# A decoder trunk with a mixture of experts: one ring of eight weight buffers, and the last norm read from PSUM

## The chip, the core and the metric

The kernel runs on one core of a Trainium2 chip. The metric is the device time of one execution in microseconds (us). The program has two layers, one after the other; all inputs and weights lie in HBM as float32, 509 MB are read in one execution.

## The reference, cut to what matters

Each layer has three sub-layers: a token mixer (short convolution beside latent attention), a cross-attention into 256 memory tokens, and a mixture of experts. After each of them the input is added and the sum is normalised. The change touches the third:

```python
D_MODEL, SEQ, DEPTH = 1024, 256, 2
N_EXPERTS, TOP_K, EXPERT_DIM = 64, 8, 256
DEEPNORM_ALPHA = (2 * DEPTH) ** 0.25

def layer_norm(x, g, b):
    mu = jnp.mean(x, axis=-1, keepdims=True)
    var = jnp.mean(jnp.square(x - mu), axis=-1, keepdims=True)
    return (x - mu) * lax.rsqrt(var + LN_EPS) * g + b

def experts(xt, gt):                     # gt: 8 of 64 gates per token are not zero
    hid = jax.nn.silu(jnp.einsum('btd,edf->btef', xt, w_gate)) * jnp.einsum('btd,edf->btef', xt, w_up)
    return jnp.einsum('btef,efd->btd', hid * gt[..., None], w_down)

def reference(x, mem, ...):
    for l in range(DEPTH):
        x = layer_norm(DEEPNORM_ALPHA * x + parallel_mixer(x, ...), ln1_g[l], ln1_b[l])
        x = layer_norm(DEEPNORM_ALPHA * x + memory_cross_attention(x, mem, ...), ln2_g[l], ln2_b[l])
        shared = (jax.nn.silu(x @ ws_gate[l]) * (x @ ws_up[l])) @ ws_down[l]
        x = layer_norm(DEEPNORM_ALPHA * x + experts(x, gates) + shared, ln3_g[l], ln3_b[l])
    return x
```

Every expert has a gate and an up matrix of 1024x256 and a down matrix of 256x1024, 1 MB each. All of them are read in each layer: 201 MB.

## The kernel before, in words

The order of the work is written out by hand, one instruction stream per engine, with semaphores between them. SP (SyncE) issues the weight loads, PE (TensorE) multiplies, ACT and DVE (VectorE) empty PSUM and do the norms, POOL (GpSimd) does small pieces of the norms.

**Dense stages.** The weights of the mixer, the cross-attention and the shared expert go through `ring`, six slots of 2 MB, in the order of `LOADS`; SP refills a slot when PE has filled the last bank that used it (`wait_read`). The 256 tokens are two blocks of 128 (`TT`), the 1024 channels eight chunks of 128 (`KC`).

**Expert stage.** The router puts the tokens of an expert into 32 slots per block. PE gathers a batch of four pairs of experts: one-hot matmuls of `x_hi` and `x_lo` (the input split into two parts) with `sel` give `xg`, L878. Then it goes pair by pair (`expert_body`, eight pairs in a body, four bodies): gate and up matmuls of both experts over eight chunks into `work[0]` (L952, 32 records a pair, 7.09 us); silu on ACT (L1169); times up and gate on DVE (L1568); two transposes (L969); down matmuls (L982); the result as `out_hi` and `out_lo` (L1173, L1579), and from these the scatter matmuls into `moe_sum`, four PSUM banks that hold the sum of the stage (L912). Gathers for the next batch and the scatter of the pair before stand between.

**Weights of the expert stage.** A pair needs three slots of 2 MB: gate and up of expert one, gate and up of expert two, down of both. In the ring these are slots 0, 1, 2 and 3, 4, 5 by turns. SP refills a gate and up slot when `gate_up_done` of the pair has come, and a down slot after `down_filled` (L474 and L480 are their issues). Each slot takes two DMAs of 1 MB: gate and up of one expert with one row of 8 KB per partition, down with two rows of 4 KB per partition. The first pair's gate and up weights lie in `ahead`, two more pieces of 2 MB in the arena, which are loaded while the dense stages end and are not used again in the layer.

**Around it.** `arena` is SBUF that stages share by views: `xg`, `ahead`, `hid` and, at its head, `gb`, the gain and bias rows of the norm. `X`, the input of the stage, has its own 8 KB per partition. After the last scatter `add_and_normalize` does, on DVE, four times `alpha * X + moe_sum` (L1239) and its statistics (L1246), then the aggregate (L1249); POOL makes the root and the shift (L578 to L594); ACT and DVE write the normalised halves `XN` (L1043, L1263), which PE transposes for the next layer (L688); DVE centres and scales (L1252) and writes the new X (L1273), which is the output after the last layer. In the loop head of the next layer ACT and DVE copy the transposed XN to `XT` (L1033, L1283). The causal mask of the attention is built on POOL once, at the start (L546, L561), and read at L1379.

## Time and profile before

| | us |
|---|---|
| three runs: median, lowest, highest | 1768.1, 1767.76, 1768.31 |
| the profiled execution | 1768.32 |
| its span, first to last instruction | 1766.5 |
| PE, PE weight loads, DVE, ACT, POOL busy | 1622.6, 909.8, 428.9, 279.9, 83.9 |
| mean granted TensorE clock | 0.984 |

The span is cut in 40 slices of 44.2 us. A digit of 9 for DMA says that the sixteen DMA engines were busy 90% of the slice or more; GB/s is what they moved. The two runs of slices near 417 GB/s are the expert stages of the two layers, 403 to 874 and 1277 to 1747 us. In the rows of a timeline the first number is the start, the second the length, in us from the span's start; in square brackets stands the idle time before and what ended it. In the chain of waits the first two numbers are the same, for merged pieces.

### The profile page before, as it was taken

The page shows a single profiled execution, that of the slowest core. Times are in us where ns is not written, and L with a number is a line of the kernel's source. Part 1 is how long each engine was busy: PE and PEld are TensorE (multiplying, and loading weights), DVE is VectorE, ACT ScalarE, POOL GpSimd, SP SyncE. Part 2 cuts the span into 40 slices and gives each one's busy share as a digit, 9 for nine tenths or more (in the row PEclk, how much of TensorE's full clock was granted, in tenths as well). Part 3 has the DMA queues.
Part 4 walks back from the last instruction along what each step waited for, and adds up shares of the span by engine and source line. Part 5 has one row for each costly group of instructions (what it writes and reads, how often), then busy time and mean ns, then how long its engine had stood idle before and what let it go on. Part 6 is the DMA issues. An engine that isn't in the chain of part 4 may idle for free.

```text
span 1766.5 us, 20370 instructions
## 1 busy us (share of the span) xinstructions
PE 1622.6 (92%) x7892; PEld 909.8 (52%) x7893; DVE 428.9 (24%) x865; ACT 279.9 (16%) x546; POOL 83.9 (5%) x121
## 2 busy tenths in 40 slices
PE   6999999989999999989789999999899999999985
PEld 4878677564333333333367885865633333333332
DVE  2141211152222222222322312011522222222224
ACT  1041011021111111111111310110211111111111
POOL 2000011040000000000010000200300000000001
PEclk8999999999999999999989999999999999999998
DMA  9174442446999999999940734333479999999994
GB/s 300 54 266 163 143 166 103 157 176 248 417 417 417 417 418 418 418 418 418 403 151 1 294 134 167 143 149 143 191 291 418 417 416 417 417 418 417 417 418 183
DMA packets 124811, 509.59 MB, mean 288 GB/s; under 512 B 12768, under 2 KB 16960, under 8 KB 91472
## 3 DMA queue, kind: packets, MB, share of 16 engines
q1 hardware_dynamic: 119808, 508.59, 72.3%
q10 hardware_dynamic: 4720, 0.02, 0.3%
q8 instruction: 46, 0.75, 0.2%
q0 software_dynamic: 224, 0.12, 0.1%
q14 instruction: 13, 0.11, 0.0%
HBM read 507.64 MB, written 1.05 MB: 288 GB/s over the span
## 4 chain that ended last, share of the span: by engine, by line
PE 65%; DMA 27%; DVE 3%; issue 2%; SPq 2%; ACT 1%; POOL 0%; ACTq 0%; DVEq 0%; POOLq 0%
PE work L662 37%; DMA ring<-in_w_up 26%; PE work L952 17%; PE work L982 4%; SPq L474 2%; PE work L878 2%; PE moe_sum L912 1%; PE moe_sum L866 1%; PE work L688 1%; PE work L756 0%; DVE stats L1246 0%; DMA par_all<-in_w_conv 0%; DVE X L1239 0%; DMA ring<-in_w_in 0%; PE work L777 0%
## 5 line engine op out<-in xcount | busy, mean ns | idle before, releaser
L952 PE MATMUL work<-ring,arena 128*64 128x512 f32 x1984 | 443.7, 599 | 62.9 <-DMA ring<-in_w_up 52.9
L952 PEld LDWEIGHTS work<-ring,arena 128*64 128x64 f32 x1984 | 157.1, 138 | 307.2 <-issue 305.1
L662 PE MATMUL work<-XT,ring 128*128 128x256 f32 x1280 | 278.2, 379 | 1.1 <-DVE arena L1379 1.1
L662 PEld LDWEIGHTS work<-XT,ring 128*128 128x128 f32 x1280 | 242.7, 190 | 35.7 <-DVE arena L1379 1.9
L982 PE MATMUL work<-ring,arena 128*64 128x512 f32 x1024 | 233.9, 598 | 1.3 <-DVE arena L1572 1.3
L662 PE MATMUL work<-ring,arena 128*128 128x512 f32 (+1 forms) x336 | 140.6, 579 | 8.3 <-DVE arena L1422 3.4
L1579 DVE TENSOR_TENSOR out_lo<-work,out_hi 128x512 fp32r<-128x512 f32 x128 | 88.6, 692 | 231.5 <-ACT out_hi L1173 231.5
L1568 DVE SCALAR_TENSOR_TENSOR arena<-arena,slot_gate,work 128x256 f32<-128x256 f32 x64 | 30.7, 480 | 449.3 <-ACT arena L1169 449.3
L982 PEld LDWEIGHTS work<-ring,arena 128*64 128x64 f32 x1024 | 68.0, 136 | 134.0 <-issue 111.3
L1173 ACT CAST out_hi<-work 128x512 fp32r<-128x512 f32 x128 | 75.1, 587 | 213.0 <-PE work L982 213.0
L1169 ACT ACTIVATE arena<-work 128x256 f32<-128x256 f32 x64 | 24.7, 385 | 523.2 <-PE work L952 523.2
L662 PEld LDWEIGHTS work<-ring,arena 128*128 128x128 f32 x336 | 63.3, 190 | 82.7 <-issue 72.9
L878 PE MATMUL work<-sel,x_hi 128*128 128x256 f32 x288 | 90.1, 335 | 1.6 <-DVE arena L1544 1.4
L878 PEld LDWEIGHTS work<-sel,x_hi 128*128 128x128 f32 x288 | 54.0, 188 | 66.6 <-issue 63.7
L578 POOL TENSOR_SCALAR small<-small 128x1 f32<-128x1 f32 x20 | 6.8, 338 | 1602.7 <-DVE small L1249 1544.9
L878 PE MATMUL work<-sel,x_lo 128*128 128x256 f32 x288 | 75.6, 285 | 0.0
L912 PE MATMUL moe_sum<-out_hi,selT 32*128 32x512 f32 x512 | 64.6, 494 | 1.8 <-DVE out_lo L1579 1.6
L912 PEld LDWEIGHTS moe_sum<-out_hi,selT 32*128 32x128 f32 x512 | 24.5, 181 | 63.6 <-issue 62.6
L662 PE MATMUL work<-ring,XT 128*128 128x384 f32 (+2 forms) x192 | 49.6, 421 | 7.9 <-DMA ring<-in_w_in 5.3
L1150 ACT COPY arena<-work 128x512 f32<-128x512 f32 x72 | 42.3, 587 | 85.8 <-PE work L878 85.8
L662 PE MATMUL work<-arena,ring 128*128 128x256 f32 x256 | 55.8, 380 | 0.0
L662 PE MATMUL work<-memT,ring 128*128 128x256 f32 x256 | 55.6, 379 | 0.0
(204 smaller groups left out, 1168.9 us busy)
## 6 DMA issues: line engine op xcount, KB each, us to landing
ring<-in_w_down SPq DMA_DIRECT2D x128, 1024.0 KB, 19.1
ring<-in_w_gate SPq DMA_DIRECT2D x124, 1024.0 KB, 15.2
ring<-in_w_up SPq DMA_DIRECT2D x124, 1024.0 KB, 17.4
ring<-in_w_in SPq DMA_DIRECT2D x28, 1024.0 KB, 12.4
ring<-in_w_mix_out SPq DMA_DIRECT2D x8, 1024.0 KB, 12.7
ring<-in_w_xk SPq DMA_DIRECT2D x8, 1024.0 KB, 6.2
ring<-in_w_xq SPq DMA_DIRECT2D x8, 1024.0 KB, 7.8
ring<-in_w_xv SPq DMA_DIRECT2D x8, 1024.0 KB, 6.2
```

The lines of the kernel that those rows point to most:

```text
L474: sp.dma_start(dst[:, h * SLOT // 2:(h + 1) * SLOT // 2].rearrange("p (k n) -> p k n", k=KC), w[at].rearrange("o p k f -> (o p) k f")).the ...
L662: mm = pe.matmul(dst, a, b, start=(k == 0), stop=(k == len(pairs) - 1))
L688: mm = pe.transpose(w[:, (c * TT + t) * P:(c * TT + t + 1) * P], XN[:, t, 2 * i + c::KC], ident[:, :])
L878: mm = pe.matmul(dst[:, :, t, :], part[:, t, c * P:(c + 1) * P], src, start=(part is x_hi), stop=(part is x_lo))
L912: mm = pe.matmul(moe_sum[2 * (q % TT) + half][:, :], selT[rows, b, k, :], part[rows, half * BANK:(half + 1) * BANK], start=False, stop=Fal ...
L952: mm = pe.matmul(work[0][rows, :], xg[b][:, c, k * P + e * TT * SLOTS:k * P + (e + 1) * TT * SLOTS], wgu[:, :, c, :], start=(c == 0), stop ...
L982: mm = pe.matmul(w[rows, :], hidT[:, c, rows], wd[:, c, half * BANK:(half + 1) * BANK], start=(c == 0), stop=(c == 1))
L1150: act.copy(xg[b][:, c, :], work[bank][:, :]).then_inc(gather_ready[0], 1)
L1169: act.activation(act_gate, work[0][:, 0:EXPERT_DIM], ACT.Silu).then_inc(silu_ready, 1)
L1173: act.copy(out_hi[:, half * BANK:(half + 1) * BANK], work[1 + half][:, :]).then_inc(hi_ready[half], 1)
L1568: dve.scalar_tensor_tensor(out=hid, in0=act_gate, scalar=slot_gate[:, b, k:k + 1], in1=work[0][:, EXPERT_DIM:2 * EXPERT_DIM], op0=ALU.mult ...
L1579: dve.tensor_tensor(out_lo[:, cols], work[1 + half][:, :], out_hi[:, cols].bitcast(F32), ALU.subtract).then_inc(lo_ready[half], 1)
```

## The change

The eight buffers (six of `ring`, two of `ahead`) form one ring of `UNITS`. A pair of experts takes three units in turn: gate and up weights of both experts for contraction chunks 0 to 3, the same for chunks 4 to 7, down of both. SP refills a unit when its reader is through, and `gate_up_done` counts halves of a pair. To have `ahead` free of other use for the whole stage, `xg`'s second buffer goes to the head of the arena (where `gb` lies, so ln3's rows are loaded after the last gate and up matmul) and a buffer `xg_more`; `hid`, `hidT` and `gated` share `hidden`, silu writes `hid` in place, and ACT waits for two DVE reads of `gated` before the fourth silu of a batch; `X` lies where `out_hi` and `out_lo` are; the mask lies in the arena and POOL builds it in each layer after the `rankT` transposes. Gates and shared hidden values are divided by alpha, so `moe_sum` holds the sum over alpha: PE adds `x_hi` and `x_lo` by identity matmuls (`add_input`, behind pairs 4 to 7 of the first body), the statistics are read from PSUM with the epsilon divided by alpha squared, ACT writes all halves of XN from PSUM, and DVE centres from PSUM, block 1 first.

The diff, cut; the hunk that moves the mask's memset and two selects into POOL's layer loop is among what is left out.

```diff
...
 RING = 6
+UNITS = 8
...
-RING_USES = BODY_PAIRS // 2
+RING_USES = 3 * BODY_PAIRS // UNITS
...
-        xg = [view(2 * K + b * 4 * K, KC, BATCH * P) for b in range(2)]
-        ahead = view(6 * K, 2, SLOT)
...
+        xg_first, xg_second = view(2 * K, KC, BATCH * P), view(0, KC // 2, BATCH * P)
+        xg = [[xg_first[:, c, :] for c in range(KC)],
+              [(xg_second if c < KC // 2 else xg_more)[:, c % (KC // 2), :] for c in range(KC)]]
+        ahead = view(6 * K, UNITS - RING, SLOT)
+        unit = [ring[:, u, :] if u < RING else ahead[:, u - RING, :] for u in range(UNITS)]
+        hid = hidden[:, 0:EXPERT_DIM]
+        hidT = hidden[:, EXPERT_DIM:].rearrange("p (c s) -> p c s", c=2)
+        gated = hidden[:, :].rearrange("p (k t) -> p k t", k=BATCH)
+        mask = view(0, 3 * P)
...
+            def wait_unit_read(m, pairs, halves):
+                q, part = divmod(m - UNITS, 3)
+                if part == 2:
+                    alone(sp, down_filled[1], pairs + (q + 1))
+                else:
+                    alone(sp, gate_up_done, halves + (2 * q + part + 1))
...
+                def load_unit(m, pair_first):
+                    u, part = m % UNITS, m % 3
+                    for i in range(2):
+                        if part == 2:
+                            dst = unit[u][:, i * SLOT // 2:(i + 1) * SLOT // 2].rearrange("p (k n) -> p k n", k=2)
+                            src = e_down[bass.ds(pair_first + i, 1)].rearrange("o p k d -> (o p) k d")
+                        else:
+                            dst = unit[u].rearrange("p (w e k n) -> p w e k n", w=2, e=2, k=KC // 2)[:, i]
+                            src = (e_gate, e_up)[i][bass.ds(pair_first, 2), :, part * (KC // 2):(part + 1) * (KC // 2), :
+                                                    ].rearrange("e p k f -> p e (k f)")
+                            dst = dst.rearrange("p e k n -> p e (k n)")
+                        sp.dma_start(dst, src).then_inc(slot_loaded[u], 16)
+                first = [sp.snap(l * EXPERTS + 2 * q) for q in range(BODY_PAIRS)]
+                for m in (0, 1):
+                    wait_read(l, len(LOADS) - RING + m)
+                    load_unit(m, first[0])
                 b, n = job("xpT", JOBS["xpT"] - 1)
                 alone(sp, filled[b], l * BANK_USES[b] + n)
...
-                def load_pair(l, i, j, pairs, gate_up=True):
-                    pair_first = sp.snap(l * EXPERTS + i * 4 + 2 * j)
-                    for e in range(2):
-                        if gate_up:
-                            sp.wait_ge(gate_up_done, pairs + (j + 1))
-                            load_gate_up(ring[:, 3 * j + e, :], pair_first + e, slot_loaded[3 * j + e])
-                    sp.wait_ge(down_filled[1], pairs + (j + 1))
-                    load_down(3 * j + 2, pair_first)
...
+                load_unit(6, first[2])
+                for m in (2, 3):
+                    wait_read(l, len(LOADS) - RING + m)
+                    load_unit(m, first[m // 3])
+                load_unit(7, first[2])
+                for m in (4, 5):
+                    wait_read(l, len(LOADS) - RING + m)
+                    load_unit(m, first[m // 3])
+                def load_body(body, pair_firsts, units):
+                    pairs, halves = sp.snap((body + 1) * BODY_PAIRS), sp.snap((body + 1) * (2 * BODY_PAIRS))
+                    for m in units:
+                        wait_unit_read(m, pairs, halves)
+                        load_unit(m, pair_firsts[m // 3])
+                load_body(base, first, range(UNITS, UNITS * RING_USES))
                 sp.reg_mov(more, 1)
-                sp.reg_mov(start, 2)
+                sp.reg_mov(start, 1)
...
                 with sp.Fori(0, more) as r:
+                    with sp.Fori(start, BODIES) as i:
+                        firsts = [sp.snap(l * EXPERTS + i * (2 * BODY_PAIRS) + 2 * q) for q in range(BODY_PAIRS)]
+                        load_body(sp.snap(base + r * BODIES + i), firsts, range(UNITS * RING_USES))
                     sp.reg_mov(start, 0)
                     alone(sp, routing_ready, l + 1)
                     sp.reg_load(more, rounds[0:1, bass.ds(l, 1)])
+                done = sp.value_load(bodies[0:1, bass.ds(l + 1, 1)], min_val=0, max_val=4 * BODIES * DEPTH)
+                alone(sp, gate_up_done, sp.snap((done + 1) * (2 * BODY_PAIRS)))
                 load_ln(l, ln3_g, ln3_b, 2)
...
+                def add_input(i):
+                    t, half = i // 2, i % 2
+                    for part in (x_hi, x_lo):
+                        rows = in_rows(part, t)[:, half * (BANK // KC):(half + 1) * (BANK // KC), :]
+                        pe.matmul(moe_sum[i][:, :].rearrange("p (q c) -> p q c", c=KC), ident_r[:, :], rows,
+                                  start=False, stop=False, skip_group_check=True)
...
+                    loaded = [pe.snap((body * RING_USES + (l + 1) * DENSE_USES) * 32), pe.snap(body * (RING_USES * 32))]
...
-                        b, k, slot = q // BATCH, q % BATCH, 3 * (q % 2)
-                        arrived = 32 * (q // 2 + 1)
-                        if first and q == 0:
-                            pe.wait_ge(ahead_loaded, l * 64 + 64)
-                        else:
-                            for e in range(2):
-                                pe.wait_ge(slot_loaded[slot + e], loaded + arrived)
+                        b, k = q // BATCH, q % BATCH
+                        def wait_unit(m):
+                            u = m % UNITS
+                            pe.wait_ge(slot_loaded[u], loaded[u // RING] + 32 * (m // UNITS + 1))
+                            return unit[u]
                         if k == 3:
                             pe.wait_ge(gated_ready, batch + (b + 2))
-                        for c in range(KC):
...
-                        mm.then_inc(gate_up_done, 1)
+                        for part in range(2):
+                            wgu = wait_unit(3 * q + part).rearrange("p (w e k n) -> p w e k n", w=2, e=2, k=KC // 2)
+                            for c in range(part * (KC // 2), (part + 1) * (KC // 2)):
+                                if k == 0:
+                                    pe.wait_ge(gather_ready[c % 2], (batch + b) * (KC // 2) + (c // 2 + 1))
+                                for e in range(2):
+                                    rows = slice(e * TT * SLOTS, (e + 1) * TT * SLOTS)
+                                    mm = pe.matmul(work[0][rows, :],
+                                                   xg[b][c][:, k * P + e * TT * SLOTS:k * P + (e + 1) * TT * SLOTS],
+                                                   wgu[:, :, e, c % (KC // 2), :], start=(c == 0), stop=(c == KC - 1))
+                            mm.then_inc(gate_up_done, 1)
...
+                        if first and q >= BODY_PAIRS - 4:
+                            add_input(q - (BODY_PAIRS - 4))
...
+                    if which == 2:
+                        if t == 1:
+                            act.wait_ge(centred_ready, l + 1)
+                        for half in range(2):
+                            act.activation(XN[:, t, half * BANK:(half + 1) * BANK], moe_sum[2 * t + half][:, :],
+                                           ACT.Identity, scale=ln_rstd[:, t:t + 1], bias=ln_shift[:, t:t + 1]
+                                           ).then_inc(norm_ready[half], 1)
+                        continue
...
+                            act.wait_ge(gate_up_done, halves + 2 * (BODY_PAIRS + q + 1))
+                            if k == 3:
+                                act.wait_ge(selT_ready, batch + (b + 2))
+                                act.wait_ge(slot_gate_ready, batch + (b + 2))
+                            act.activation(hid, work[0][:, 0:EXPERT_DIM], ACT.Silu).then_inc(silu_ready, 1)
...
-                    w = wait_filled(dve, l, stage, i) if stage else moe_sum[2 * t + half]
-                    ins = dve.scalar_tensor_tensor(out=X[:, t, cols], in0=X[:, t, cols], scalar=ALPHA, in1=w[:, :],
-                                                   op0=ALU.mult, op1=ALU.add)
                     if stage:
-                        take(ins, l, stage, i)
-                    else:
-                        step(ins)
-                    settle()
-                    step(dve.bn_stats(stats[:, t, 6 * half:6 * half + 6], X[:, t, cols]))
+                        w = wait_filled(dve, l, stage, i)
+                        take(dve.scalar_tensor_tensor(out=X[:, t, cols], in0=X[:, t, cols], scalar=ALPHA, in1=w[:, :],
+                                                      op0=ALU.mult, op1=ALU.add), l, stage, i)
+                        settle()
+                    step(dve.bn_stats(stats[:, t, 6 * half:6 * half + 6],
+                                      X[:, t, cols] if stage else moe_sum[2 * t + half][:, :]))
...
-                def centre(t):
-                    return dve.scalar_tensor_tensor(out=centred[:, t, :], in0=X[:, t, :],
-                                                    scalar=moments[:, 2 * t:2 * t + 1], in1=gb[:, 0, :],
-                                                    op0=ALU.subtract, op1=ALU.mult)
-                if which == 2:
-                    dve.wait_ge(ln_loaded, (l * 3 + 3) * 32)
-                    settle()
-                    step(centre(0))
...
+                dve.wait_ge(ln_loaded, (l * 3 + 3) * 32)
+                settle()
+                for t in (1, 0):
+                    if t == 0:
+                        for half in range(2):
+                            dve.wait_ge(norm_ready[half], l * 6 + 7)
+                    for half in range(2):
+                        cols = slice(half * BANK, (half + 1) * BANK)
+                        ins = dve.scalar_tensor_tensor(out=centred[:, t, cols], in0=moe_sum[2 * t + half][:, :],
+                                                       scalar=moments[:, 2 * t:2 * t + 1], in1=gb[:, 0, cols],
+                                                       op0=ALU.subtract, op1=ALU.mult)
+                        if t == 1 and half == 1:
+                            tell(ins, centred_ready, l + 1)
+                        else:
+                            step(ins)
+                settle()
                 for t in range(TT):
...
+                    dve.wait_ge(ln_rstd_ready, l * 6 + (5 + t))
+                    tell(dve.scalar_tensor_tensor(out=X[:, t, :], in0=centred[:, t, :], scalar=ln_rstd[:, t:t + 1],
+                                                  in1=gb[:, 1, :], op0=ALU.mult, op1=ALU.add),
+                         (layer_done if t == 0 else ln_applied), (l + 1 if t == 0 else l * 3 + 4))
...
```

## Rows read from the trace of the kernel before

**Rows 1.** The page, 40 slices: DMA busy tenths, GB/s

```profile
DMA  9174442446999999999940734333479999999994
GB/s 300 54 266 163 143 166 103 157 176 248 417 417 417 417 418 418 418 418 418 403 151 1 294 134 167 143 149 143 191 291 418 417 416 417 417 418 417 417 418 183
```

**Rows 2.** Waits, whole span: who waited for whom, us in total, times, longest

```profile
PE work L952 <- DMA ring<-in_w_up: 52.9, 39, 2.8
```

**Rows 3.** The chain of waits: pairs 0 and 4 of the first layer

```profile
403.24 7.04 PE work L952 x32
...
457.99 7.02 PE work L952 x32
```

**Rows 4.** Timeline, 398 to 436 us, PE: pairs 0 and 1

```profile
403.17 7.09 PE L952 MATMUL work<-arena 128*64 128x512 f32 x32
...
416.62 7.09 PE L952 MATMUL work<-ring,arena 128*64 128x512 f32 x32
```

**Rows 5.** Timeline of SP's queue, 340 to 520 and 830 to 856 us

```profile
397.37 19.57 SPq L480 DMA_DIRECT2D ring<-in_w_down  x4
423.89 0.34 SPq L474 DMA_DIRECT2D ring<-in_w_gate  x1
...
845.95 1.54 SPq L449 DMA_DIRECT2D arena<-in_ln_g  x1
```

**Rows 6.** DMA, 400 to 440 us, 40 slices of 1 us

```profile
GB/s 430 406 426 418 111 0 0 0 0 0 0 0 0 0 0 0 0 156 373 430 410 422 307 0 66 139 426 451 418 410 401 426 451 401 426 393 430 418 397 422
```

**Rows 7.** DMA of 527.5-530.9, 617.86-621.26, 517.6-525.8 and 884-892 us, in turn

```profile
DMA packets 359, 1.41 MB, mean 413 GB/s; under 512 B 20, under 2 KB 20, under 8 KB 355
...
DMA packets 356, 1.39 MB, mean 408 GB/s; under 512 B 19, under 2 KB 19, under 8 KB 354
...
DMA packets 469, 3.40 MB, mean 415 GB/s; under 512 B 52, under 2 KB 52, under 8 KB 57
...
DMA packets 1455, 3.11 MB, mean 388 GB/s; under 512 B 47, under 2 KB 47, under 8 KB 1454
```

**Rows 8.** Timeline, 860 to 900 us: the end of the first layer

```profile
860.70 7.09 PE L952 MATMUL work<-ring,arena 128*64 128x512 f32 x32 [1.04 <-DMA ring<-in_w_up]
...
869.95 3.65 PE L982 MATMUL work<-ring,arena 128*64 128x512 f32 x16
...
877.38 0.69 DVE L1239 SCALAR_TENSOR_TENSOR X<-X,moe_sum 128x512 f32<-128x512 f32 x1 [1.68 <-PE moe_sum L912]
...
880.14 0.21 DVE L1249 BATCH_NORM_AGGREGATE small<-stats 128x2 f32<-128x12 f32 x1
...
881.87 0.24 POOL L594 TENSOR_SCALAR small<-small 128x1 f32<-128x1 f32 x1
...
887.42 0.81 ACT L1043 ACTIVATE arena<-X,small 128x512 f32<-128x512 f32 x1 [4.47 <-POOL small L594]
...
888.60 1.28 DVE L1273 SCALAR_TENSOR_TENSOR X<-arena,small 128x1024 f32<-128x1024 f32 x1
```

**Rows 9.** Timeline of the second layer's stage: first, last gate/up, last norm

```profile
1276.78 7.09 PE L952 MATMUL work<-arena 128*64 128x512 f32 x32
...
1734.24 7.09 PE L952 MATMUL work<-ring,arena 128*64 128x512 f32 x32 [1.04 <-DMA ring<-in_w_up]
...
1762.15 1.28 DVE L1273 SCALAR_TENSOR_TENSOR X<-arena,small 128x1024 f32<-128x1024 f32 x1
```

**Rows 10.** Groups by line: busy us, mean ns | idle before, what ended it

```profile
L878 PE MATMUL work<-sel,x_hi 128*128 128x256 f32 x288 | 90.1, 335 | 1.6 <-DVE arena L1544 1.4
L1102 ACT ACTIVATE arena<-work 128x512 f32<-128x512 f32 x8 | 4.8, 598 | 50.5 <-PE work L662 50.5
```

**Rows 11.** The mask: its selects by line (POOL), its first reader in time

```profile
L561 POOL TENSOR_SCALAR_AFFINE_SELECT mask<-mask 128x128 f32<-128x128 f32 x2 | 0.5, 294 | 0.0
...
120.07 2.52 DVE L1379 TENSOR_TENSOR arena<-work,mask 128x384 f32<-128x384 f32 x4 [0.95 <-PE work L762]
```

163 lines of the change are left out of this document (63 added, 100 removed).

## The prediction

> **What bounds the kernel now.** I read the slices of the page first [rows 1]: in slices 10 to 18 and 30 to 38 the DMA digit is 9 and the rate lies at 416 to 418 GB/s; these are the two expert stages. In the dense stages the rate is 54 to 300 and PE carries the time. So an expert stage is a stream of weights, and the question is when the stream starts, how fast it runs, and what is left to do when it ends. The table of waits agrees: PE waits only 52.9 us in all for a weight load, in 39 short waits [rows 2], so PE lags the stream by little: four pairs of experts take PE 457.99 - 403.24 = 54.75 us when nothing is missing, 13.7 us each [rows 3], and the stream needs 6.29 MB / 417 GB/s = 15.1 us each. 32 pairs are 438 us of PE and 483 us of stream; the stage ends early enough only because eight 2 MB pieces are there at its start.
>
> The start is where the stream loses time. The last dense slot is refilled from 397.37 on, and the next issue that brings new weights in earnest is at 423.89, after the second pair's gate and up matmuls; between them one w_down piece goes out when the first pair's down matmuls end [rows 4, 5]. The DMA view of 400 to 440 us shows it: 0 GB/s from 405 to 417, one burst, another hole at 423 to 425, then full rate [rows 6]. The reason is in the code: the two pieces that hold the first pair's gate and up weights lie in the arena (`ahead`) and are never used again, so the ring works with six.
>
> **Part 1, the ring of eight.** The change keeps the two arena pieces in the ring and cuts a pair into three units of 2 MB: gate and up of both experts for contraction chunks 0 to 3, the same for 4 to 7, and down. SP can refill unit 0 when the first half of the first pair's matmuls is through: they start at 403.17 and take 7.09 us, so half is at 406.7, and SP issues 0.18 us after such an end (416.62 + 7.09 = 423.71 to 423.89) [rows 4, 5], at 406.9. The later units come free faster than the stream takes them (PE 13.7 us for three, stream 15.1 or more), so from there it need not pause. Before the last matmul half, 87 units have to land (8 of the 96 are there, the last down follows).
>
> How long is a unit? Gate and up now come as rows of 4 KB where they were 8 KB; down was and is 4 KB. The stream of before has both kinds by turns. Of seven stretches with 4 KB packets nearly alone the first ran at 413 GB/s and the last at 408, the others between; of the 8 KB stretches beside them the slowest ran at 415 [rows 7]. A stretch holds some packets of its neighbour, which pulls both kinds together, so I take 410 for 4 KB, below the middle: 2.097 MB / 410 = 5.115 us a unit, against 5.03 at the stream's 417. The ends are 415 (5.05 us, 5.4 us less a layer) and 408 (5.14 us, 2.2 us more). What stands around the stream I take from before: from the issue at 423.89 to the last gate and up landing at 860.70 [rows 5, 8] are 436.8 us with 86 pieces of 5.03 (432.6), so 4.2 us are first latency and last landing. After: 406.9 + 87 x 5.115 + 4.2 = 856.1. Then only half of the gate and up matmuls is left, 3.55 us: end at 859.65, against 860.70 + 7.09 = 867.8. That is 8.1 us earlier. The last down unit lands at 861.2; its matmuls came 2.16 us after the gate and up matmuls (867.79 to 869.95) [rows 8], now at 861.8, so it is just in time, by 0.6 us; what it is late beyond that, the end is late too.
>
> In the second layer the stage starts at 1276.78 and the last matmuls at 1734.24 [rows 9]: 1276.78 + 3.55 + 0.18 + 445.0 + 4.2 = 1729.7, end 1733.3, against 1741.3: 8.0 us.
>
> The Trainium skill (DMA: Bandwidth & Descriptors, Anatomy of one DMA) fits a transfer as 2.0 us plus bytes over 436 GB/s, with nothing for the size of the rows. By it the unit would not grow, and the sum would be that of rival B, 1729.6. The trace leans against it, by little.
>
> **Part 2, the input through PE.** Eight matmuls of 128x512 per layer with an identity are added behind pairs 4 to 7 (of 32). The nearest rows are the gathers, 335 ns for 256 columns [rows 10]: 8 x 2 x 0.335 = 5.4 us at most, 2 to 3 likely since such records overlap. All of it lies beside a stream that is already the slower side; by pair 4 PE leads by 4 x 1.4 = 5.6 us against the refill that the stream needs next. Cost 0; if that cover were gone, up to 5.4 us a layer. The strided moving operand has no row here; twice the price would still fit.
>
> **Part 3, the last norm.** Before: four times add (0.69) and statistics (0.69), then centre, scale, final; from the first add at 877.38 to the end of the last L1273 at 889.88 are 12.5 us [rows 8]; at the end of the kernel it is the same chain, ending at 1763.43 [rows 9]. After, on DVE: four statistics straight from PSUM 2.8, two aggregates 0.45, two halves of centring for block 1 from PSUM 1.35, the same for block 0 1.35, two L1273 2.55: 8.5 with the gaps. ACT must do block 0's XN before the second centring: its POOL chain ends 1.8 us after the aggregate (880.35 to 882.11) [rows 8], so at 880.8, and two halves from PSUM at 0.6 (as L1102) [rows 10] end at 882.0, the moment DVE wants them. So 3.9 us less. Bounds: 0 if PSUM reads or POOL hold it, 4.7 if ACT's XN, which ends at 888.23 now and at 883.5 then, were the gate; but it is DVE that, after its last L1273 [rows 8], must come round to the next layer and copy half of XT before PE can go on, so I take DVE's 3.9. At the end of the kernel the output DMA moves by the same.
>
> **Part 4, the small moves.** The ln3 rows are loaded only when the last gate and up matmul is done, 859.7, instead of from 845.95 on [rows 5]; two 0.5 MB loads behind the last down unit land near 867, and DVE wants them at 880.7 - 8.1 = 872.6: hidden by 5 us. The next layer's six dense loads stand behind them on SP, some 8 us later than now, six units of 5.4 us at the 388 GB/s of such rows [rows 7]: the first is there by 873. PE needs it after the transposes of XN, which follow ACT's at 888.23 [rows 8] less 12 us, so not before 876; and the dense stages draw less than the queue gives in every slice [rows 1]. Cost 0; the cover is 3 us, and if it failed, its lack would be the cost. The mask is made once per layer on POOL (two selects of 0.29 us and a memset) once rankT is transposed, before the q and k projections, and DVE reads it at 120.07 [rows 11]: hidden by PE work of tens of microseconds. ACT's two more waits before the fourth silu of a batch are for DVE work that precedes 7 us of PE matmuls: 0.
>
> **Sum.** 8.1 + 8.0 + 2 x 3.9 = 23.9 us off the profiled execution's 1768.3 (span 1766.5 and 1.8 around it; the median 1768.1 is the same number): 1744.
>
> **Rivals.**
> A, as worked out: 1744, its own range 1737 to 1752.
> B, rows of 4 KB cost nothing: unit 5.03, 87 x 0.085 = 7.4 us less a layer, 1744.4 - 14.8 = 1729.6. For it: the two kinds lie within 2% and their windows are blurred. PE does not stop it: 403.2 + 31 x 13.7 + 3 loop turns of 1.5 us reach the last pair by 832.
> C, the stream gains as in A but the new norm gives nothing, because ACT and DVE take turns at PSUM and each waits for the other: 1752.
> D, the other side. A gate or up load now takes every other 4 KB of a matrix, for two experts by turns; if HBM or the queue serves that worse, it hits 58 of the 87 units. Priced with the only slower rate in the trace, 388 GB/s for the 2 KB rows of w_in [rows 7]: 5.405 us, 58 x 0.29 = 16.8 us a layer more, 4.8 more than all gains: 1744 + 33.6 = 1778. It decides from 5.32 us a unit, 394 GB/s. Against it: down loads also read rows 0.5 MB apart by turns, and keep 408 or more [rows 7].
>
> **How the numbers follow.** A 0.57, B 0.13, C 0.15, D 0.10, and 0.05 for something between. About 0.2% (3.5 us) is what a measurement of this kernel can tell from no change. A, B and C are all far beyond it: faster 0.87; D slower 0.10; 0.03 between. The range runs from B's time to beyond C's, 1728 to 1757, and leaves out D.
>
> **What would show it.** In the trace after: no hole at 405 to 417 and none behind it; 409 to 411 GB/s through slices 10 to 18 (417 means B, under 395 D); PE waits of 1.5 us twice in a pair or less; the last gate and up matmul at 859 to 860; about 8.5 us from the end of the scatters to the last L1273 (12 means C). The prediction is wrong if a hole stays at the start of the stage, or if the stream's rate leaves 408 to 416.

## The result: 1.0% faster, three quarters of the forecast gain

| | median us (lowest to highest) | ratio to before, 95% interval |
|---|---|---|
| before, on the same chip | 1768.2 (1767.76 to 1769.27) | |
| changed | 1750.59 (1750.04 to 1752.47) | 0.990 (0.9887 to 0.9914) |
| forecast | 1744 | 0.986 |

The gain is 17.6 us where 23.9 were forecast; between the two profiled executions it is 18.2 us (spans 1766.5 and 1748.3).

The page of the changed kernel comes first: the span, two of the rows of slices, and the packets. It is to be laid beside [rows 1].

```profile
span 1748.3 us, 20830 instructions
...
DMA  9164343448999999999870734434599999999995
GB/s 298 60 258 175 125 164 127 145 164 337 409 409 409 409 409 409 410 410 410 333 282 1 293 140 168 145 128 166 192 359 409 409 409 409 410 410 409 409 410 232
DMA packets 157587, 509.65 MB, mean 292 GB/s; under 512 B 12768, under 2 KB 16960, under 8 KB 157008
```

Through both stages the rate is 409 to 410 where it was 416 to 418. The bytes are the same; now nearly every packet is under 8 KB. The tenth slice, in which the first stage begins, moved 337 GB/s for 248 before, because the stream starts earlier. The DMA view of 400 to 440 us, one number per us, answers to [rows 6]:

```profile
GB/s 426 422 426 352 8 0 0 70 127 430 414 410 426 414 430 328 315 369 328 332 356 410 434 406 418 414 422 410 406 414 401 406 401 422 410 406 397 426 410 406
```

The two holes of 12 and 2 us are gone; what is left is 404 to 409, until the first refill (issued at 406.79) arrives. New is a dip, 315 to 369 GB/s at 415 to 421. The next rows are the timeline of the first layer's stage: its start, its last gate and up half, its last down matmuls, and then the turn to the next layer; they answer to [rows 3, 8].

```profile
402.96 7.09 PE L976 MATMUL work<-ring,arena 128*64 128x512 f32 x32
...
859.25 3.65 PE L976 MATMUL work<-arena,xg_more 128*64 128x512 f32 x16 [0.97 <-DMA arena<-in_w_up]
...
863.15 0.35 SPq L459 DMA_DIRECT2D arena<-in_ln_g  x1
...
865.07 3.65 PE L1006 MATMUL work<-arena,hidden 128*64 128x512 f32 x16
...
872.48 1.29 DVE L1286 BATCH_NORM_STATS2 stats<-moe_sum 128x6 f32<-128x512 f32 x2 [1.66 <-PE moe_sum L937]
...
875.85 0.21 POOL L578 TENSOR_SCALAR small<-small 128x1 f32<-128x1 f32 x1
...
877.36 1.41 DVE L1309 SCALAR_TENSOR_TENSOR arena<-moe_sum,small,arena 128x512 f32<-128x512 f32 x2 [0.49 <-ACT arena L1074]
877.45 1.45 ACT L1074 ACTIVATE arena<-moe_sum,small 128x512 f32<-128x512 f32 x2 [0.19 <-POOL small L610]
878.89 2.48 DVE L1319 SCALAR_TENSOR_TENSOR X<-arena,small 128x1024 f32<-128x1024 f32 x2
...
885.67 0.18 DVE L1337 COPY par<-par_all 128x17 f32 x1 [4.30 <-issue]
886.00 1.90 DVE L1328 TENSOR_SCALAR XT<-work,par 128x256 f32<-128x256 f32 x4 [0.16 <-DVE par L1337]
...
887.05 8.43 PE L678 MATMUL work<-ring,XT 128*128 128x384 f32 x21 [2.76 <-DVE XT L1328]
```

The second layer, from timelines of its start and end, beside [rows 9]:

```profile
1266.55 5.80 PE L976 MATMUL work<-ring,arena 128*64 128x512 f32 x26
...
1722.97 3.65 PE L976 MATMUL work<-arena,xg_more 128*64 128x512 f32 x16 [0.97 <-DMA arena<-in_w_up]
...
1736.19 1.29 DVE L1286 BATCH_NORM_STATS2 stats<-moe_sum 128x6 f32<-128x512 f32 x2 [1.65 <-PE moe_sum L937]
...
1742.60 2.48 DVE L1319 SCALAR_TENSOR_TENSOR X<-arena,small 128x1024 f32<-128x1024 f32 x2
```

From these ends the gain adds up. In the kernel before, the next layer's L662 resumed at 896.74.

| stretch | before | after | gain | forecast |
|---|---|---|---|---|
| stage 1, first gate/up matmul to end of the last | 464.6 | 459.9 | 4.7 | 8.1 |
| its end to the next layer's matmuls | 28.95 | 24.15 | 4.8 | 3.9 |
| dense part of layer 2 | 380.0 | 379.5 | 0.5 | 0 |
| stage 2 | 464.6 | 460.1 | 4.5 | 8.0 |
| its end to the end of the span | 25.2 | 21.7 | 3.5 | 3.9 |
| start of stage 1 | 403.2 | 403.0 | 0.2 | 0 |
| sum | | | 18.2 | 23.9 |

So the norm gave what was forecast, and a little more; the stage gave only 4.7 of 8.1.

### The profile page after: what moved, and what is told of

The parts are those of the page before. It is cut to its first block, busy times and chain, and to the rows that moved or that the text cites. A ratio compares the mean times of both kernels' runs of the same rounds, so it can differ in the third digit from the quotient of the medians.

```text
span 1748.3 us, 20830 instructions
## 1 busy us (share of the span) xinstructions
PE 1631.3 (93%) x7908; PEld 888.5 (51%) x7909; DVE 420.4 (24%) x858; ACT 282.4 (16%) x550; POOL 80.1 (5%) x124
## 3 DMA queue, kind: packets, MB, share of 16 engines
HBM read 507.64 MB, written 1.05 MB: 291 GB/s over the span
## 4 chain that ended last, share of the span: by engine, by line
PE 59%; SPq 29%; DMA 5%; issue 3%; DVE 2%; ACT 1%; DVEq 0%; ACTq 0%; POOL 0%; POOLq 0%
PE work L678 38%; SPq L502 29%; PE work L976 9%; PE work L1006 5%; DMA arena<-in_w_up 4%; PE work L894 2%; PE moe_sum L937 2%; PE moe_sum L882 1%; PE work L704 1%; PE moe_sum L929 0%; PE work L772 0%; DMA par_all<-in_w_conv 0%; DMA ring<-in_w_in 0%; PE work L993 0%; PE work L793 0%
## 5 line engine op out<-in xcount | busy, mean ns | idle before, releaser
L976 PE MATMUL work<-ring,arena 128*64 128x512 f32 x1152 | 260.0, 597 | 16.2 <-DMA ring<-in_w_up 12.9
L1006 PE MATMUL work<-ring,hidden 128*64 128x512 f32 x768 | 175.4, 599 | 1.0 <-DVE hidden L1620 1.0
L976 PEld LDWEIGHTS work<-ring,arena 128*64 128x64 f32 x1152 | 77.7, 136 | 169.8 <-issue 139.9
L1616 DVE SCALAR_TENSOR_TENSOR hidden<-hidden,slot_gate,work 128x256 f32<-128x256 f32 x64 | 30.8, 481 | 440.9 <-ACT hidden L1210 440.9
L1210 ACT ACTIVATE hidden<-work 128x256 f32<-128x256 f32 x64 | 24.6, 385 | 514.7 <-PE work L976 514.7
L976 PE MATMUL work<-ring,xg_more 128*64 128x512 f32 x384 | 87.1, 595 | 17.6 <-DMA ring<-in_w_up 17.6
L1006 PEld LDWEIGHTS work<-ring,hidden 128*64 128x64 f32 x768 | 51.0, 136 | 100.5 <-issue 85.1
L976 PE MATMUL work<-arena 128*64 128x512 f32 x384 | 86.8, 597 | 6.6 <-DMA arena<-in_w_up 5.9
L578 POOL TENSOR_SCALAR small<-small 128x1 f32<-128x1 f32 x20 | 4.8, 238 | 1505.3 <-DVE small L1290 1446.8
L976 PEld LDWEIGHTS work<-ring,xg_more 128*64 128x64 f32 x384 | 26.5, 137 | 76.1 <-issue 48.0
L1006 PE MATMUL work<-arena,hidden 128*64 128x512 f32 x256 | 58.5, 599 | 0.0
## 6 DMA issues: line engine op xcount, KB each, us to landing
ring<-in_w_mix_out SPq DMA_DIRECT2D x8, 1024.0 KB, 12.5
```

The lines of the kernel that those rows point to most:

```text
L976: mm = pe.matmul(work[0][rows, :], xg[b][c][:, k * P + e * TT * SLOTS:k * P + (e + 1) * TT * SLOTS], wgu[:, :, e, c % (KC // 2), :], start ...
L1006: mm = pe.matmul(w[rows, :], hidT[:, c, rows], wd[:, e, c, half * BANK:(half + 1) * BANK], start=(c == 0), stop=(c == 1))
L1210: act.activation(hid, work[0][:, 0:EXPERT_DIM], ACT.Silu).then_inc(silu_ready, 1)
L1616: dve.scalar_tensor_tensor(out=hid, in0=hid, scalar=slot_gate[:, b, k:k + 1], in1=work[0][:, EXPERT_DIM:2 * EXPERT_DIM], op0=ALU.mult, op1 ...
```

## Experiments

All were timed in three rounds beside runs of the kernel before on the same chip (its medians 1768.4 and 1769.2). The changed kernel was not timed beside them, so a difference to its 1750.6 can be off by the 1.0 us by which the kernel before differs between chips (1768.2 beside the changed kernel). T is the theory of the prediction: half a row of 4 KB costs 2% of rate, the earlier refill pays that and more, and the added matmuls are hidden. What "the stage" gains is read as above, from the first layer.

**1. Units by expert, rows of 8 KB (e1_expert_units).** The ring of eight stays, only the cut of a unit changes:

```diff
-                            src = (e_gate, e_up)[i][bass.ds(pair_first, 2), :, part * (KC // 2):(part + 1) * (KC // 2), :
-                                                    ].rearrange("e p k f -> p e (k f)")
+                            src = (e_gate, e_up)[i][bass.ds(pair_first + part, 1)].rearrange("o p k f -> (o p) k f")
```

> The changed kernel with one edit: a pair's two gate and up units are split by expert again (each one expert's gate and up matrices, rows of 8 KB), not by contraction half. Ring of eight, norm and all else stay. Theory T (a row of 4 KB costs the stream 2%, and the first refills of the half units run thin): no dip after the first refill, 417 GB/s in the stage, first refill at 410.3 us instead of 406.8, the last gate and up matmuls start near 852.5 and take 7.1, end near 859.5 where the changed kernel has 862.9: 3.4 us a layer less, 1744 in all. Rival R (the rate of 409 comes with eight buffers and their deeper queue, or from both experts' rows by turns, not from the row length): the rate stays 409, 87 x 5.12 = 445.6 from 410.3 on, end near 868: 1761.

Measured: 1743.74 (1743.57 to 1743.97), ratio 0.9859 (0.9843 to 0.9876), 6.9 us under the changed kernel. Below are the windows of the steady part and the DMA view of 400 to 440 us:

```profile
500.00:840.00 340.00, 319.34 (x1746) 126.79 (x1746) 80.41 (x141) 53.41 (x99) 0.00 (x0) 1.00 1.02 417
...
GB/s 406 422 410 434 266 8 0 0 0 0 0 53 127 406 422 414 426 463 401 410 475 418 401 410 442 451 401 348 401 414 430 393 442 397 410 475 418 401 401 442
```

The rate is the last number of the first row. It is 417 again and there is no dip, though the first refill (410.81) waits for the whole first pair and so starts 4.0 us later than in the changed kernel (3.4 us against the start of the stage). The stage takes 456.6 us (403.56 to 860.2), 3.3 less than in the changed kernel: whole rows are worth more than the earlier start. The time is what theory T said, 1744.

**2. The kernel before with every row in two 4 KB pieces (e2_before_4k).** Ring of six, same order; only the packets change:

```diff
-                        sp.dma_start(dst[:, h * SLOT // 2:(h + 1) * SLOT // 2].rearrange("p (k n) -> p k n", k=KC),
-                                     w[at].rearrange("o p k f -> (o p) k f")).then_inc(loaded, 16)
+                        sp.dma_start(dst.rearrange("p (g w n) -> p g w n", g=2, w=2)[:, :, h, :],
+                                     w[at].rearrange("o p (g k) f -> (o p) g (k f)", g=2)).then_inc(loaded, 16)
```

> The kernel before with one edit: gate and up rows of 8 KB are written as two pieces of 4 KB (the slot's layout is half, matrix, chunk), so every packet of the expert stage is 4 KB; ring of six, same loads, same order, the two halves of a row one after the other. Theory T: 409 GB/s in the stage; 86 pieces x (5.12 - 5.03) = 7.8 us a layer, 1784 in all. Rival R (row length costs nothing, the half rows' stride or the alternation of two experts or the deeper ring did it): 417 GB/s and 1768.

Measured: 1784.97 (1784.39 to 1787.01), ratio 1.0096 (1.0079 to 1.0113): 16.6 us slower than before. The window of the steady part, and the last gate and up matmuls of layer 1 (860.70 in before):

```profile
500.00:840.00 340.00, 301.53 (x1654) 124.00 (x1652) 75.42 (x133) 50.07 (x93) 0.00 (x0) 1.00 1.03 409
...
869.64 2.79 PE L952 MATMUL work<-ring,arena 128*64 128x512 f32 x12 [1.33 <-DMA ring<-in_w_up]
```

The same 409 GB/s as in the changed kernel. With a stream that sets the end, rows of 4 KB cost 8.9 us a layer by themselves. Rival B, by which they cost nothing, falls.

**3. The norm part alone (e3_norm_only).** The kernel before, with `add_input`, the scaling by alpha, statistics and centring from PSUM, and nothing else. The core of its edit:

```diff
+                    step(dve.bn_stats(stats[:, t, 6 * half:6 * half + 6],
+                                      X[:, t, cols] if stage else moe_sum[2 * t + half][:, :]))
...
+                        if first and q >= BODY_PAIRS - 4:
+                            add_input(q - (BODY_PAIRS - 4))
```

> The kernel before with only the second part of the change: input added to the sums by PE, statistics, XN and centring from PSUM, gates and shared values over alpha; ring of six, old units, mask at the start. Theory T: the stage is as long as before (the eight added matmuls hidden), the tail is 4.5 us shorter at the layer's turn and 3.5 at the end of the kernel: 1760. Rival N (PE is so close to the stream in the first bodies of the ring of six that the added matmuls push the refills, which wait for PE there): 1 to 3 us a layer given back, 1763 to 1766.

Measured: 1761.02 (1758.29 to 1761.58), ratio 0.9954 (0.9937 to 0.997), 7.4 us under before. Timeline of layer 1:

```profile
405.13 3.23 PE L968 MATMUL work<-arena 128*64 128x512 f32 x14
...
862.66 3.65 PE L968 MATMUL work<-ring,arena 128*64 128x512 f32 x16 [1.05 <-DMA ring<-in_w_up]
...
893.90 6.39 PE L669 MATMUL work<-ring,XT 128*128 128x384 f32 x19 [3.06 <-DVE XT L1314]
```

From first to last gate and up matmul are 457.53 us; before it was 860.70 - 403.17 = 457.53 too. So the added matmuls cost the stage nothing. From the last of these matmuls to the next layer's are 31.24 us, before 896.74 - 860.70 = 36.04: 4.8 us, as in the changed kernel. Rival C falls, and with it the thought that PE's added work ate the stage's gain.

**4. Gate of both experts, then up of both (e4_gate_then_up).** This keeps the early first refill and has rows of 8 KB. Unit one of a pair holds two gate matrices, unit two the two up matrices, and PE does 64 matmuls of 256 columns for 32 of 512:

```diff
+                            src = (e_gate, e_up)[part][bass.ds(pair_first + i, 1)].rearrange("o p k f -> (o p) k f")
...
+                            cols = slice(part * EXPERT_DIM, (part + 1) * EXPERT_DIM)
...
+                                    mm = pe.matmul(work[0][rows, cols],
```

> The changed kernel with its half units cut another way: unit one is the gate matrices of both experts, unit two the up matrices, so rows are 8 KB again and a unit is still free after half of the matmuls; a pair takes twice as many matmuls of half the columns (256), with as many more weight loads. Theory T (row length is what costs): 417 GB/s, first refill at 406.9, 87 x 5.03 = 437.6 and 4.2 to 6.8 around it, the last half ends between 852.3 and 854.9 where the split by expert ends at 860: 11 to 16 us less than its 1743.7, 1728 to 1733. Rival P (weight loads of 138 ns can't hide behind 110 ns of matmul, so PE takes 64 x 0.138 = 8.8 us instead of 7.1 for a pair's gate and up, 15.4 a pair, more than the stream's 15.1): PE is the bound, no waits for loads, 32 x 15.4 = 493 us for a stage: 1775 or more.

Measured: 1735.41 (1735.14 to 1736.73), ratio 0.9812 (0.9795 to 0.9828), 15.2 us under the changed kernel. Timeline of the first pair and of the last halves; the window; the DMA view of 400 to 440 us:

```profile
404.26 7.13 PE L975 MATMUL work<-ring,arena 128*64 128x256 f32 x64
...
852.74 1.95 PE L975 MATMUL work<-arena 128*64 128x256 f32 x16 [0.54 <-DMA arena<-in_w_up]
...
500.00:840.00 340.00, 327.72 (x2530) 180.00 (x2528) 81.11 (x142) 53.42 (x100) 0.00 (x0) 0.99 1.02 416
...
GB/s 299 418 422 393 451 45 0 0 0 123 369 414 410 430 451 418 434 442 410 418 410 434 434 401 389 397 422 410 410 434 418 430 418 442 393 426 434 418 426 393
```

Twice as many weight loads take PE hardly more time: 7.13 us against 7.09 for the first pair. The rate is back, there is no dip, and the stage takes 452.1 us, 7.8 less than in the changed kernel. T named the direction and the mechanism; the time is above its band by 2.4 us.

**5. The same, with w_down in rows of 8 KB too (e5_gate_then_up_down8).** A partition takes two neighbouring rows of w_down, and the transposes take every other column of `hid`:

```diff
-            e_down = w_down.rearrange("l e (k p) d -> (l e) p k d", p=P)
+            e_down = w_down.rearrange("l e (p k) d -> (l e) p k d", p=P)
...
-                            mm = pe.transpose(work[0][:, c * P:(c + 1) * P], hid[:, c * P:(c + 1) * P], ident[:, :])
+                            mm = pe.transpose(work[0][:, c * P:(c + 1) * P], hid[:, c::2], ident[:, :])
```

> The kernel before this one with one more edit: w_down is laid out so that a partition holds two neighbouring rows (8 KB in one piece), and the transposes of the hidden values take every other column. Theory T: every packet of the stage is 8 KB, 421 GB/s, 4.975 us a unit; 88 x 0.05 = 4.4 us less a layer than the kernel before it, 1719 to 1725. Rival P: PE is the bound there already, no gain from the stream. Rival R (the two kinds of packets differ for another reason than length, such as where w_down lies): 417 and no gain.

Measured: 1728.7 (1727.9 to 1730.56), ratio 0.9773 (0.9756 to 0.9789): the best version, 21.9 us under the changed kernel, but 3.7 above the upper end of T's band. Its window:

```profile
500.00:840.00 340.00, 333.69 (x2566) 184.47 (x2564) 82.02 (x144) 54.40 (x102) 0.00 (x0) 0.98 1.01 421
```

With all weights in rows of 8 KB the stream runs at 421 GB/s. In the profiled executions the two stages take 447.9 and 448.1 us, 4.3 and 4.4 less than in experiment 4; the rates alone would give some 9 in both, so the stages gain what they should. The whole gains 6.2 there (spans 1734.9 and 1728.7), because the dense part of layer 2 is 2.6 us longer (382.8 for 380.2): its first 10 us ran at a granted clock of 0.69, for 0.83 in experiment 4. PE has little idle time by now, 333.7 of 340 us busy against 320.7 in the changed kernel (its window of the same stretch).

**6. The changed kernel with w_down alone in rows of 8 KB (e6_down8).** The two edits of experiment 5 to w_down and `hid`, on the changed kernel.

> The changed kernel with the w_down edit alone: gate and up halves stay at 4 KB rows, down rows are 8 KB. Theory T: 29 down units at 4.975 instead of 5.12 us: 4.2 us less a layer, 413 GB/s in the stage, 1742. Rival R (not the row length of w_down): 409 GB/s and 1750.6.

Measured: 1745.0 (1742.87 to 1746.87), ratio 0.9867 (0.9851 to 0.9884), 5.6 us under the changed kernel; T had the rate right and the time 3 us too low. The window, and the DMA view of 400 to 440 us:

```profile
500.00:840.00 340.00, 323.27 (x1752) 123.27 (x1750) 80.41 (x141) 53.35 (x99) 0.00 (x0) 1.00 1.02 413
...
GB/s 426 451 418 418 33 16 0 0 131 393 451 418 442 369 381 303 344 336 360 315 319 393 430 430 434 422 430 434 414 418 418 397 393 406 418 414 397 410 418 434
```

A third of the units in long rows gives a third of the rate between 409 and 421. The dip stays (413 to 422), so the rows of w_down are not what makes it.

**7. The first refill held for the whole first pair (e8_late_first).** This asks what the dip and the fixed part are made of. Q: the dip comes from the queue being thin after the first refill, and a later, denser start loses less than the delay. F: the whole delay comes back at the end.

```diff
+                alone(sp, gate_up_done, sp.snap((base + 1) * (2 * BODY_PAIRS) + 2))
```

> The changed kernel, but SP holds its first refill of a layer's expert stage until both halves of the first pair are done (one more wait, first issue at 410.3 instead of 406.8); nothing else. It asks for the 3.1 us a layer by which the forecast of the stage was short. Theory Q (the first refills came one at a time, each alone in the queue, and ran at 330 GB/s from 415 to 421: 1.5 us lost, which a later, fuller start does not lose): the stage ends 1.9 to 2.2 us later, 1754.6. Rival F (that dip is no loss of its own, every issue's delay goes to the end in full): 3.5 us later in each layer, 1757.6.

Measured: 1760.72 (1759.21 to 1761.21), ratio 0.9953 (0.9936 to 0.9969). The timeline, SP's first issue, PE's last half; then the DMA view:

```profile
404.53 3.65 PE L977 MATMUL work<-ring,arena 128*64 128x512 f32 x16
...
411.94 0.95 SPq L502 DMA_DIRECT2D ring<-in_w_down  x2
...
865.32 3.65 PE L977 MATMUL work<-arena,xg_more 128*64 128x512 f32 x16 [0.94 <-DMA arena<-in_w_up]
...
GB/s 180 414 422 410 426 193 0 0 0 0 0 0 12 160 397 418 393 414 410 430 369 336 328 287 324 319 356 397 430 410 442 385 406 422 406 418 410 406 397 422
```

Neither: 3 us above F, 6 above Q. Against the stage's start the first refill is 3.6 us later in both layers, and the last half 4.5 us later in the first and 5.7 in the second. So the delay comes back in full and 1 to 2 us more, and the dip is there as before, 5 us later. Q falls. It also shows what the earlier refill is worth in the changed kernel, 4.5 and 5.7 us. Why it is more than the delay is open.

**8. Half rows without turns (e10_half_rows_alone).** Each gate or up load of the changed kernel fetches half rows of two experts by turns. Here each is two loads of 0.5 MB, one expert each (the w_down loads are halved too, which the lines below leave out): A says that the turns make the dip, H that the half rows do.

```diff
+                        for e in range(2):
...
+                                at = (2 * i + e) * SLOT // 4
+                                dst = unit[u][:, at:at + SLOT // 4]
+                                src = (e_gate, e_up)[i][bass.ds(pair_first + e, 1), :,
+                                                        part * (KC // 2):(part + 1) * (KC // 2), :
+                                                        ].rearrange("o p k f -> (o p) (k f)")
```

> The changed kernel, one edit: every load of 1 MB in the expert stage is two of 0.5 MB, one expert each, so the half rows (4 KB of every 8) of one expert come alone, none by turns. Same rows of 4 KB, same units. Theory A: no dip, 409 GB/s from the first refill on; twice the number of loads costs the stream nothing or little; 1747 to 1751. Rival H (half rows): the dip stays at 415 to 421 and in the first loads, 1750.6 or, if twice the loads cost something, more.

Measured: 1751.64 (1751.23 to 1752.05), ratio 0.9902 (0.9885 to 0.9918), as the changed kernel. DMA view of 400 to 440 us:

```profile
GB/s 332 348 373 340 410 201 29 0 0 90 356 418 373 414 430 397 356 246 410 287 299 233 361 418 426 418 426 418 406 414 418 397 406 410 414 401 418 406 414 401
```

The dip is there (416 to 422), and deeper, down to 233. The turns are not needed for it; H stands.

**9. Rows of both experts by turns, 8 KB (e9_alternate_rows).** Experiment 4, but with each of a unit's two DMAs taking half the partitions and both experts, instead of all partitions and one expert. It was to show the turns alone.

```diff
+                            half = slice(i * P // 2, (i + 1) * P // 2)
+                            dst = unit[u][half].rearrange("p (e n) -> p e n", e=2)
+                            src = (e_gate, e_up)[part][bass.ds(pair_first, 2), half].rearrange("e p k f -> p e (k f)")
```

> The kernel with gate units and up units (8 KB rows, 1735.4 us), one edit: a unit's two loads are cut by partitions (0 to 63, 64 to 127), and each takes rows of both experts by turns, as the changed kernel's loads do; rows stay whole, 8 KB. It asks where the changed kernel's dip to 330 GB/s at 415 to 421 us, and the same rate in its first loads at 364 to 370 us, come from. Theory A (rows of two experts, 1 MB apart, by turns are slow to fetch while the sixteen engines run in step): the dip is back, 1 to 2 us a layer, 1738. Rival H (it is the half rows, 4 KB of every 8): no dip, 1735.

Measured: 2569.44 (2518.27 to 2585.27), before 1769.24 beside it. Both theories missed by 830 us. The DMA view of 500 to 560 us, 1.5 us a number:

```profile
GB/s 208 213 229 213 213 224 218 210 205 216 229 388 410 229 205 218 218 216 210 213 218 208 213 224 213 199 224 202 232 366 388 194 224 194 238 210 199 221 213 218
```

The rate is 194 to 238 while gate and up loads run, and 366 to 410 in the short stretches in which the w_down loads, which are as in experiment 4, are under way. So it is the form of these loads that halves the rate. Two things differ from experiment 4, the half of the partitions and the turns; no run takes them apart. The changed kernel has such turns on all partitions, in rows of 4 KB, and keeps 409, which leaves the half of the partitions as the likelier cause, not shown. The experiment does not answer its question.

## Why the prediction was right, and where its size was off

**The hole at the start: right.** The first refill followed the first half of the pair. In the changed kernel it goes out at 406.79 (forecast 406.9), and experiment 7 shows that delaying it by 3.6 us costs 4.5 and 5.7.

**The rate of 4 KB rows: right, 409 for the 410 taken.** It was the choice on which most hung, and the prediction took it from seven blurred stretches [rows 7]. Experiment 2 gives the same 409 on the kernel before, experiments 4 and 5 give 416 and 421 for fewer such rows. A unit is 2.097 MB / 409 = 5.128 us, 0.0126 more than forecast, 1.1 us over 87 units. The fit of the Trainium skill (DMA: Bandwidth & Descriptors, Anatomy of one DMA) was made on loads that GpSimd issues, while SP issues them here; having no term for the size of the rows, it would put these runs at one rate. They are at four: 409, 413 (experiment 6), 416 to 418 and 421.

**The term that was mis-sized: "first latency and last landing", 4.2 us.** In the changed kernel from the first refill's issue to the last half are 859.25 - 406.79 = 452.5 us; less 87 x 5.128 = 446.1 they leave 6.4, which is 2.2 more than forecast. With the 1.1 of the rate and 0.1 in the length of the last half (3.65 for 3.55), that is the 3.4 us missing in the stage. Of the 2.2 the dip accounts for about half: six microseconds at a mean of 338 GB/s instead of 410 lose 1.05 us. The step failed in taking the fixed part from a kernel whose loads have another shape [rows 5, 6]. Rival D named this shape, half rows of two experts, but priced it in all 58 units. What is true of D is some microseconds at the start; in the steady part the rate is the same 409 as in experiment 2, where whole rows are taken in two pieces.

Most of the rest is at the end of the stream. When the last half starts, the weight queue has moved 183.92 MB since the first refill's issue, and 87 units are 182.45: 1.47 MB, 3.6 us of stream, belong to the last w_down unit, which the half does not need. The same sum gives 1.17 MB, 2.8 us, in the kernel before (181.52 MB from 423.89 to 860.70, for 86 units). That is 0.8 us. The DMA view of 850 to 870 us of the changed kernel shows how such a stream ends, 0.5 us a number:

```profile
GB/s 401 393 426 410 418 426 401 401 401 393 426 410 410 434 401 401 401 303 303 270 229 180 156 156 66 57 25 8 106 311 385 361 426 360 107 57 0 0 16 0
```

From 858.5 on the rate runs down over 5 us, with nothing queued behind the last w_down unit: some of the engines seem to be through well before others. So they work on the last unit while others still bring the one before it. Why this lead is larger than in the kernel before was not tried.

The experiments fit. By the same reckoning the fixed part is 4.8 us in experiments 1 and 2, 5.4 in 4 and 5.2 in 5, the four without the dip, and 6.7, 7.3 and 6.4 in 6, 7 and 8, which have it. For 4 and 5 the rate has to be the weights' own, 415.4 and 419.3 GB/s from 430 to 840 us: with twice as many matmuls 0.48 MB of instructions were loaded in that time, against 0.13 in the changed kernel, and they are in the 416 and 421. A rate that is wrong by 0.5 GB/s moves a fixed part by 0.5 us, so the tenths between these kernels mean little.

**The last down unit: on time.** Its matmuls came 2.17 us after the end of the last gate and up matmuls (862.90 to 865.07), as in before. The cover of 0.6 us held.

**The input through PE: hidden, as forecast.** All eight matmuls of a group have the same length; the view by line of them:

```profile
L929 PE MATMUL moe_sum<-x_hi,ident_r x8: 716/722/723, 470.9 to 1378.7; 128*128 128x512 f32 x8
```

The 722 ns compare with the bound of 2 x 335 = 670 from the gathers, so the strided operand costs little. The first two of them hold PE for 1.14 us from start to start (470.91 to 472.05), so the eight take some 4.6 us a layer: under the bound of 5.4, but more than the 2 to 3 called likely. Experiment 3 shows that they cost the stage nothing.

**The norm: right.** From the first statistics to the end of the last L1319 are 881.37 - 872.48 = 8.9 us, forecast 8.5, before 12.5. The difference is about the wait that the sum had at nothing: ACT's two halves took 1.45 us where 1.2 were taken, and DVE waited 0.49 us for them before its second L1309. Another 1.2 us came at the turn of the layer: the gap before DVE's first instruction there is 4.30 us, before 5.48; what shortens it is not shown. Together they are the 4.8 of the first layer; at the end of the kernel only the first is left, 3.5. What the prediction did not see is what POOL does in the kernel before. Its timeline of the second block's chain, with DVE beside it:

```profile
883.22 1.28 DVE L1252 SCALAR_TENSOR_TENSOR arena<-X,small,arena 128x1024 f32<-128x1024 f32 x1
883.38 1.20 POOL L578 TENSOR_SCALAR small<-small 128x1 f32<-128x1 f32 x1 [1.27 <-DVE small L1249]
...
886.01 1.28 DVE L1273 SCALAR_TENSOR_TENSOR X<-arena,small 128x1024 f32<-128x1024 f32 x1
886.12 1.27 POOL L594 TENSOR_SCALAR small<-small 128x1 f32<-128x1 f32 x1
```

Beside a DVE instruction with two operands of full length in SBUF these operations on one number per partition take POOL 1.20 and 1.27 us; in the first block's chain the same two took 0.21 (at 880.54) and 0.24 [rows 8]. In the changed kernel DVE's L1309 reads one of them from PSUM, and none of POOL's operations beside it is stretched (L578 takes 0.21 at 875.85, with L1309 under way from 875.45 to 876.86). So POOL's chain for block 1 hardly holds ACT up any more: ACT's wait for it is 0.19 us where it was 4.47 [rows 8]. What this adds to the gain beyond DVE's own chain is not shown.

**The small moves: free, as forecast.** The ln3 rows are asked for at 863.15, and DVE's first use of them at 875.45 waited for nothing.

**The rivals.** A was the right one, 6.6 us above its forecast and inside its own range. B falls with experiments 1 and 2, C with experiment 3, D as priced with the 409 GB/s of the steady part.

## What to carry to other kernels

Once a stream of loads sets the end, count its rows as well as its bytes: going from 8 KB to 4 KB rows cost up to 3% of rate here (421 to 409 GB/s), and of the 12.5 us that the ring of eight brought a stage with whole gate and up rows (experiment 4: 452.1 us for 464.6) half rows left 4.7. When a unit has to be smaller so that it comes free sooner, cut it where the rows stay whole (by matrix, as in experiment 4) and let PE pay with more, shorter matmuls; here it paid 0.04 us a pair. And the fixed part around a stream is a term like the others: take it from loads of the same shape, or give it a range, and when two kernels are compared by their rate, count the weights' own bytes, without the instruction loads.

## What the hardware showed that was not expected

- Loads over half the partitions, rows of two matrices by turns, ran at 194 to 238 GB/s, half the rate that the same bytes have over all partitions (experiment 9). The Trainium skill (DMA: Bandwidth & Descriptors, Rules for kernel authors) says that splitting a transfer over disjoint partition halves gains nothing because both halves use the same engines. Here it lost half; whether the halves alone do it, without the turns, no run shows.
- Loads that take 4 KB of every 8 KB run slowly for six to nine microseconds soon after the engines have been idle (303 to 381 GB/s in the changed kernel and experiment 6, down to 287 in 7 and 233 in 8), and at 409 from then on. Loads that take both halves of a row, in one piece or two, do not show it (experiments 1, 2, 4). Why it passes is open.
- When loads pile up in the queue, SP is held at its issues. These two rows of the changed kernel's timeline are one issue of 1 MB and two (2.36 us each); in a free queue, at 410.31, one takes 0.37:

```profile
838.76 2.06 SPq L502 DMA_DIRECT2D arena<-in_w_gate  x1
...
843.47 4.72 SPq L502 DMA_DIRECT2D arena<-in_w_down  x2
```

  It is not the 4 KB packets alone: in experiment 5, with rows of 8 KB only, two issues take 0.81 us at 491.99, but 4.12 at 824.27, late in the stage. In the changed kernel two already take 3.19 at 490.46. Nothing waits for SP there, since the queue is full meanwhile; a kernel that issues small urgent loads from the same engine would feel it.
